# Layer 1's heads: two more jobs of each period run as one 512-column matmul of the high weights plus one of the low weights

## The reference, cut to what matters

```python
for l in range(DEPTH):                       # DEPTH = 2, D_MODEL = 2048, T = 256 tokens
    h = rms_norm(x, norm_g[l])
    z = h @ w_in[l]                          # q, k, v and gate of 16 heads of 128 columns
    ...                                      # 6 dilated heads ("dil"): rope on q and k
    ...                                      # 6 neighbourhood heads ("na"), 4 memory heads ("mem")
    mk, mv = jnp.split(mem_n @ w_mem_kv[l], 2, axis=-1)
    ...
    y = jnp.concatenate([o_na * silu(na_g), o_dl * silu(dl_g), o_m * silu(m_g)], axis=-1)
    x = x + y @ w_out[l]
```

## Time and profile before

| what | value |
|---|---|
| median of 3 runs (lowest, highest) | 2434.28 us (2433.3, 2437.17) |
| the profiled execution: time, span | 2435.06 us, 2433.4 us |
| mean granted TensorE clock, share of full | 0.997 |
| TensorE busy, weight loads busy | 2404.1 us, 2173.7 us |
| VectorE, ScalarE, GpSimd busy | 1712.9, 1223.4, 527.3 us |

### The profile page before, as it was taken

One profiled execution on the slowest core, in us unless ns is written; L12 is line 12 of the kernel. 1 busy time (PEld: TensorE's weight loads), 2 busy tenths in 40 slices (PEclk: granted clock), 3 DMA queues, 4 the chain that ended last, 5 costly groups with the idle time before them and its releaser, 6 DMA issues.

```text
span 2433.4 us, 45170 instructions
## 1 busy us (share of the span) xinstructions
PE 2404.1 (99%) x15288; PEld 2173.7 (89%) x15288; DVE 1712.9 (70%) x2649; ACT 1223.4 (50%) x1838; POOL 527.3 (22%) x1003
## 2 busy tenths in 40 slices
PE   8999999999999999999999999999999999999999
PEld 7888888989999999999999999998888888888888
DVE  8977776668888887678888875666555555555555
ACT  5455454455666665566665444444444444444442
POOL 2310032246767773210011221111000000000000
PEclk9999999999999999999999999999999999999999
DMA  7765566656666665555557876766777677777774
GB/s 243 218 201 198 189 216 209 188 184 202 198 204 209 200 196 179 187 185 196 167 189 245 262 219 223 228 201 179 204 191 191 191 192 190 190 190 192 190 190 147
DMA packets 257100, 485.07 MB, mean 199 GB/s; under 512 B 23688, under 2 KB 171860, under 8 KB 256736
## 3 DMA queue, kind: packets, MB, share of 16 engines
q1 hardware_dynamic: 216064, 415.66, 56.2%
q10 hardware_dynamic: 29632, 35.30, 4.5%
q0 software_dynamic: 11296, 32.68, 4.4%
HBM read 455.20 MB, written 31.08 MB: 200 GB/s over the span
## 4 chain that ended last, share of the span: by engine, by line
PE 85%; DVE 8%; issue 3%; ACT 3%; DMA 0%; ACTq 0%; DVEq 0%; SPq 0%; POOL 0%; POOLq 0%
PE z_ps L2191 14%; PE z_ps L2179 9%; PE z_ps L2181 9%; PE z_ps L2180 9%; PE z_ps L2192 7%; PE z_ps L2590 7%; PE z_ps L2591 7%; PE z_ps L2596 7%; DVE w_lo L1393 3%; ACT w_hi L753 1%; PE o_ps L2234 1%; PE s_ps L2216 1%; PE p_ps L2626 1%; PE o_ps L2626 1%; PE v_ps L2626 1%
## 5 line engine op out<-in xcount | busy, mean ns | idle before, releaser
L1393 DVE TENSOR_TENSOR w_lo<-w_raw,w_hi 128x1024 fp32r<-128x1024 f32 x518 | 638.9, 1262 | 221.4 <-ACT w_hi L753 219.5
L753 ACT ACTIVATE w_hi<-w_raw 128x1024 fp32r<-128x1024 f32 x518 | 529.4, 1050 | 243.1 <-PE z_ps L2192 130.3
L2050 DVE TENSOR_TENSOR w_lo<-w_raw,w_hi 128x1024 fp32r<-128x1024 f32 x262 | 320.8, 1226 | 300.5 <-ACT w_hi L1233 300.2
L2191 PE MATMUL z_ps<-x_both,w_hi 128*128 128x512 f32 x1440 | 517.9, 402 | 6.7 <-DVE w_lo L1393 3.5
L1233 ACT ACTIVATE w_hi<-w_raw 128x1024 fp32r<-128x1024 f32 x262 | 277.9, 1061 | 415.3 <-PE z_ps L2596 267.8
L2179 PE MATMUL z_ps<-x_both,w_hi 128*128 128x256 f32 x1376 | 398.5, 290 | 7.2 <-DVE w_lo L1393 6.5
L2192 PE MATMUL z_ps<-x_both,w_lo 128*128 128x256 f32 x1440 | 404.1, 281 | 0.0
L2181 PE MATMUL z_ps<-x_both,w_lo 128*128 128x256 f32 x1376 | 390.5, 284 | 0.0
L2180 PE MATMUL z_ps<-x_both,w_hi 128*128 128x256 f32 x1376 | 390.4, 284 | 0.0
L2191 PEld LDWEIGHTS z_ps<-x_both,w_hi 128*128 128x128 f32 x1440 | 271.8, 189 | 70.5 <-issue 7.1
L2179 PEld LDWEIGHTS z_ps<-x_both,w_hi 128*128 128x128 f32 x1376 | 265.0, 193 | 11.8 <-issue 10.1
(11 more groups left out here) (464 smaller groups left out, 4183.9 us busy)
## 6 DMA issues: line engine op xcount, KB each, us to landing
w_raw<-in_w SPq DMA_DIRECT2D x624, 512.0 KB, 4.3
w_raw<-in_w SPq DMA_DIRECT2D x160, 256.0 KB, 3.3
w_raw<-in_w SPq DMA_DIRECT2D x80, 384.0 KB, 4.9
w_raw<-in_w SPq DMA_DIRECT2D x80, 128.0 KB, 3.0
tab_d<-arena ACTq DMA_DIRECT2D x32, 256.0 KB, 2.9
res<-tab_d POOLq DMA_DIRECT2D x16, 384.0 KB, 5.6
arena<-tab_d POOLq DMA_DIRECT2D x16, 384.0 KB, 5.8
tab_d<-arena ACTq DMA_DIRECT2D x32, 128.0 KB, 2.5
```

The costliest lines, as they stand in the source:

```text
L753: act.activation(w_hi[:, n % RING, :], w_raw[:, n % RING, :], ACT.Copy).then_inc(w_hi_ready, 1)
L1393: dve.tensor_tensor(w_lo[:, n % RING, :], w_raw[:, n % RING, :], w_hi[:, n % RING, :].bitcast(F32), ALU.subtract).then_inc(w_lo_ready, 1)
L2050: dve.tensor_tensor(w_lo[:, k % RING, :], w_raw[:, k % RING, :], w_hi[:, k % RING, :].bitcast(F32), ALU.subtract).then_inc(w_lo_ready, 1)
L2191: pe.matmul(z[:], wh, both[:, :, kt, :], start=(first and kt == kts[0]), stop=False)
```

## The change

`z_job` now always takes `job_joined`, and all evacuations of layer 1 pass `joined=True`; the counts of the semaphore `z_added` (`added`, `x3_block`) follow. It touches two jobs in each of 15 periods: 480 k-tiles, in each of which two 256-column matmuls of `w_hi` become one of 512 columns. VectorE gets 30 TENSOR_REDUCE.

```diff
         def added(p, c, l=0):
-            return 4 * p + c + 1 if l == 0 else 4 * HEADS + 2 * (p - PERIODS_LAYER) + c + 1
+            return 4 * (p if l == 0 else HEADS + p - PERIODS_LAYER) + c + 1
...
                 if kind == "dil":
-                    evac_rope(q_t[:], p, 0, l, h, 0, l == 0 or norm, norm)
+                    evac_rope(q_t[:], p, 0, l, h, 0, True, norm)
                 else:
-                    evac(k_t[:] if kind == "mem" else q_t[:], p, 0, rstd_m[:] if kind == "mem" else rstd[:], l == 0)
+                    evac(k_t[:] if kind == "mem" else q_t[:], p, 0, rstd_m[:] if kind == "mem" else rstd[:], True)
...
                 if kind == "dil":
-                    evac_rope(k_t[:], p, 1, l, h, 1, l == 0 or norm, norm)
+                    evac_rope(k_t[:], p, 1, l, h, 1, True, norm)
                 else:
-                    evac(v_t[:] if kind == "mem" else k_t[:], p, 1, rstd_m[:] if kind == "mem" else rstd[:], l == 0)
+                    evac(v_t[:] if kind == "mem" else k_t[:], p, 1, rstd_m[:] if kind == "mem" else rstd[:], True)
...
-                dve.wait_ge(z_added, added(HEADS, 0) + 2 * HEADS + n + 2)
+                dve.wait_ge(z_added, 8 * HEADS + n + 1)
...
                 def z_job(c, of_mem, wait_kt=None):
-                    if l == 0 or norm or c >= 2:
-                        pe.wait_ge(z_free, 4 * p + c + 1)
-                        job_joined(z_ps[c], p, c, m_both if of_mem else x_both, wait_kt)
-                    else:
-                        job(p, c, m_hi if of_mem else x_hi, m_lo if of_mem else x_lo, wait_kt)
+                    pe.wait_ge(z_free, 4 * p + c + 1)
+                    job_joined(z_ps[c], p, c, m_both if of_mem else x_both, wait_kt)
```

## The result

The changed kernel takes 2444.09 us (2441.55 to 2448.14) beside 2435.43 us (2433.3 to 2437.17) for the kernel before on the same chip: ratio 1.0038, 95% interval [1.0026, 1.005]. It is 8.7 us slower, beyond the 0.2% that can be told from no change. The profiled execution spans 2442.4 us, that of before 2433.4.

A forecast was written before the change was run, and what follows sets the result against it. Bound in dil periods by TensorE and an equally long VectorE-ScalarE circle; 6.7 + 0.7 - 1.0 = +6.4 us on the profiled 2435.06 gives 2441.5, or 2440.7 against the median 2434.28; own range 2439.2 to 2443.5, 8-in-10 range 2433.5 to 2446.

The forecast's parts named there:

- TensorE's gain: Joined jobs 0 and 1 in layer 1: 0.2 to 0.4 us a period, taken as 0.3, where TensorE does not wait.
- What bounds the dil heads: Heads 1 to 5: VectorE and ScalarE run a circle as long as TensorE's period, without slack for two 0.72 us reduces.
- announced waits: Heads 2 to 5: TensorE waits at L2225 for L1483 and at L2257 for L1418, about 2 us a head.
- (a): Rival: VectorE has over 1.44 us of true slack in dil periods, TensorE's gain comes through, 2429.8 us; chance 0.12.
- the circle: VectorE and ScalarE wait on each other in dil periods, 26.65 us a round, growing to 28.1 with the reduces.
- The sum at head 6: Delay from the dil heads' reduces: VectorE 6.9 us late at head 6, less 0.2 of TensorE's slack, +6.7 us.
- the three rope operations cost the same: Rope evacuations: L1441 takes 0.42 us from summed tile or bank, so each evacuation grows by the reduce's 0.72 us only.
- the smaller fixed cost of SBUF: Skill's rule weighed for the rope: each operation 0.065 us shorter on the summed tile, forecast some 1.7 us lower.
- Na and mem periods: Reduces fit partly into VectorE's idle time: +0.7 us over six na periods, -1.0 us over the mem periods.
- (b): Rival: same mechanism, but dil heads cost about 5.5 us or na heads give time back, 2434 to 2439; chance 0.18.
- (c): Rival: waits cool TensorE's clock, some 1.5 us a fall, or na heads go on losing; +9.7, 2444 us; chance 0.10.
- na heads at their upper bound: Six na periods cost +2.5 us in place of the +0.7 taken.

The follow-up runs named there:

- e5: Against the kernel before: layer 1's jobs 0 and 1 joined on TensorE, no reduce, no added semaphore instruction, one product left out; 2432.69 us, ratio 0.9985.
- e2: The changed kernel with its reduces, but jobs 0 and 1 of layer 1 back to three 256-column matmuls a k-tile (first k-tile aside); 2444.6 us, ratio 1.004.
- e10: The kernel before with the change in job 0 of the dil heads (1 to 5) alone; 2441.1 us, ratio 1.002.
- e11: The kernel before with the change in job 1 of the dil heads (1 to 5) alone; 2439.76 us, ratio 1.0017.
- e6: The changed kernel with the reduce of each rope evacuation in layer 1 issued twice; 2450.17 us, ratio 1.0061 to the kernel before.
- e8: The kernel before with the change in both jobs of the mem heads and job 0 of the na heads; 2434.76 us, ratio 0.9995.
- e12: The kernel before with the change in both jobs of the na and mem heads, none in dil heads; 2436.15 us, ratio 1.0005.
- e7: The changed kernel, reduces kept, but layer 1's rope operations read the bank's first half instead of the summed tile; 2441.06 us, ratio 1.0022 to the kernel before.
- e3: The kernel before with the change in both jobs of the dil heads (1 to 5) alone; 2444.68 us, ratio 1.0042.
- e9: The changed kernel with 8 unread matmuls ahead of L2225 in heads 2 to 5, to keep TensorE's clock up; 2444.61 us, ratio 1.0039 to the kernel before.
- e1: Against the kernel before: layer 1's jobs 0 and 1 joined, no reduce, a semaphore-only VectorE instruction added to each unjoined evacuation; 2433.87 us, ratio 0.9995.

## Why the prediction was right, and which term was too small

The forecast was +6.4 us, the measured change is +8.7. The time of 2444.09 us lies in the range of 2433.5 to 2446, but 0.6 us above the forecast's own 2439.2 to 2443.5; the kernel before now has a median of 2435.43, 1.2 us above the one that the forecast was set against.

**TensorE's gain** (0.2 to 0.4 us, taken 0.3 a period) was right: 0.29 and 0.25 in e5.

**What bounds the dil heads** was right, and is what decides: two engines full, one seen waiting. e2 shows the loss without any change on TensorE, e10 and e11 show that each reduce counts, e6 that a further one does. The announced waits of 2 us a head were 1.5 (6.1 us at L2225 and L2257 from 570 to 705 us, those put down to GpSimd among them). The distance of the first `w_lo` of neighbouring dil periods, forecast at 28.1 us, was 28.5 to 29.4. Here is that `w_lo` in heads 2 and 6, VectorE in order of time, the kernel before:

```profile
578.73 2.42 DVE L1393 TENSOR_TENSOR w_lo<-w_raw,w_hi 128x1024 fp32r<-128x1024 f32 x2 [1.85 <-ACT w_hi L753]
...
686.56 2.57 DVE L1393 TENSOR_TENSOR w_lo<-w_raw,w_hi 128x1024 fp32r<-128x1024 f32 x2 [2.20 <-ACT w_hi L753]
```

and the changed kernel:

```profile
579.67 2.61 DVE L1393 TENSOR_TENSOR w_lo<-w_raw,w_hi 128x1024 fp32r<-128x1024 f32 x2 [1.85 <-ACT w_hi L753]
...
695.77 2.56 DVE L1393 TENSOR_TENSOR w_lo<-w_raw,w_hi 128x1024 fp32r<-128x1024 f32 x2 [2.20 <-ACT w_hi L753]
```

The four periods grow by 8.27 us (e8 and e12, with the dil code of before, show 108.61 and 109.10 for them where this trace has 107.83, so the growth is known to about 1 us), and the idle time ahead of this instruction does not shrink by any of it: 1.85, 1.90, 2.28, 1.90 and 2.20 us in heads 2 to 6 before, 1.85, 1.90, 2.28, 1.89 and 2.20 now. It moves with VectorE's own work, as the prediction said against (a). The prediction took the circle from one period, 26.65 us; the four together give 26.96 a period.

**The sum at head 6** (+6.7 us) was the term that was mis-sized. L2257 of head 6 starts at 713.20 in the changed kernel and at 704.32 before, +8.9; at head 5 it is 685.16 and 677.78, +7.4 where 5.55 was forecast. Counted from L2225 of head 1, which starts 0.9 us earlier in the changed kernel's trace, it is +9.8 at head 6. Two parts are missing in the term. First, 0.72 us from the reduce to its reader was read from head 2 of layer 0, which is written out; heads 2 to 5 of layer 1 run in a loop. There the distance to the rope is 0.81 us, and the trace of before had shown it in layer 0's loop:

```profile
129.41 0.68 DVE L1418 TENSOR_REDUCE arena<-z_ps 128x256 f32<-128x512 f32 x1
130.22 0.43 DVE L1441 TENSOR_TENSOR arena<-arena 128x256 f32<-128x256 f32 x1
```

That is 8 x 0.09 = 0.7 us. All ten reduces followed by a rope in the changed layer 1 divide by it, 0.72 in head 1 and 0.81 to 0.82 in heads 2 to 5. The loop alone is not the cause, for in the same loop a reduce and its reader L1425 stay 0.71 to 0.72 us apart (the changed kernel, head 2's job 2):

```profile
604.47 0.68 DVE L1418 TENSOR_REDUCE arena<-z_ps 128x256 f32<-128x512 f32 x1
605.18 0.42 DVE L1425 TENSOR_TENSOR arena<-arena,rstd 128x256 f32<-128x256 f32 x1
```

The rope has a second wait with a register in front of it (L1439), L1425 has not. That this wait costs the 0.09 us was not tried apart. Second, "the three rope operations cost the same" held only while GpSimd rests: by the groups above, 8 x (40 + 43 + 45) ns = 1.0 us, and L1483, which comes at another place beside GpSimd, 8 x 96 ns = 0.8 us. With 8 reduces this makes 8 x 0.81 + 1.0 + 0.8 = 8.3 us for the four periods, beside the 8.27 of the `w_lo` rows, and 6.7 + 0.7 + 1.0 + 0.8 = 9.2 at head 6, beside 8.9 or 9.8. Distances are good to about 1 us, so the agreement is closer than the rows can bear out. Other operations moved too: in the same groups L1512 and L1510 grew by 0.6 and 0.4 us over 8, and L1425 and L1509 shrank by 0.6 and 0.2. That the reduces cost more than 0.72 us each is shown, the split of the excess is argued.

The Trainium skill (SBUF — State Buffer, SBUF: two separate sides) says that a VectorE operation with two SBUF inputs and a GpSimd operation that reads SBUF exclude each other on one port pair, for the whole instruction. The trace agrees on which operations are slowed, and not on how much: 0.10 to 0.18 us are lost beside GpSimd operations of 0.41 and 0.59 us. The other rule of the Trainium skill that was weighed (VectorE: DVE Perf Modes, The TRN2 errata), the smaller fixed cost of SBUF, has found nothing for it: 0.42 us either way, in e7 too.

**Na and mem periods** (+0.7 and -1.0) were right: +0.68 and, over the three periods between rows, -0.66. That the first agrees to the last digit is luck: four traces with the na heads of before or nearly so (before, e3, e10, e11) lie between 159.49 and 159.83.

**The rivals.** (a) and (b) are out by the time. The first half of (c) happened, the clock fell after waits of 1.68 and 1.89 us, and its price was nil within what can be told, as e9 shows and as the text had allowed for; its second half, na heads at their upper bound of +2.5 us, did not. The time lies near (c)'s 2444 for another reason. The 1.5 us that (c) puts on a fall stood on no row; in the changed kernel five k-tiles from 657.68 us on take TensorE 3.20 us, and five from 661.26 on 1.76, so 1.4 us of its own time.

## What to carry to other kernels

When one engine is busy all the time, ask whether a second one runs a circle of equal length beside it: then work taken from the first gains nothing and work given to the second is paid in full (e5's dil heads gained nothing, its 3 us came from na and mem heads; e2 lost 9.5). Such a circle shows by its distance between equal instructions, not by its busy share (71%) and not by its idle brackets, since these may end by a chain that starts at the engine itself. Read the price of an operation where its surroundings are those of the new place: the same waits in front of its reader, its reader behind it or not, GpSimd at work or not.

## What the runs showed of the hardware

- Operations of VectorE with both inputs in SBUF take up to 0.60 us in place of 0.42 while GpSimd works; with one input in a PSUM bank they don't change (before and e7).
- The next operation starts 0.61 us after the same reduce when it doesn't read it (e6), 0.72 when it does, and 0.81 where the reader is the rope in a loop; a reader with one wait less in front of it stays at 0.72 in the same loop.
- An instruction on VectorE that does nothing but count up a semaphore put 0.57 us between two starts in place of 0.45 (e1).
- After waits of TensorE of 1.89 and 1.68 us in the changed kernel the granted clock fell: the two stretches of 3 us behind each had a mean of 0.75 and 0.69, and 0.75 and 0.68. The trace of before showed no fall after a wait of 1.61 us. The length of the wait alone does not decide it: e3 kept 1.00 after one of 1.89 us (head 2), and e2 kept 1.00 after 1.81 us (head 2) and fell to 0.72 after 1.45 us (head 3).
